# The recurrent unit's square root on GpSimd instead of ScalarE, with its factor in the next product

## The chip, the cores and the metric

The kernel runs on one core of a Trainium2 chip. A core has TensorE (PE in the profile), VectorE (DVE), ScalarE (ACT), GpSimd (POOL) and SyncE (SP), each with an instruction queue of its own, and 16 DMA engines. What is compared is the device time of one execution, in microseconds; less is better.

## What is computed

One inference step through two layers of a hybrid backbone, on 128 context tokens and 256 latent tokens with 1024 features. Each layer has a combined input projection, attention, a recurrent branch, a gated merge of the two and a mixture of 16 experts. The part that matters here is the recurrent branch:

```python
def _rglru_bidir(xr, lp, h0):
    xc = _conv_centred(xr, lp['conv_w'], lp['conv_b']).astype(F32)
    for d in range(2):
        r = jax.nn.sigmoid(_block_diag(xc, lp['lru_wa'][d], lp['lru_ba'][d]))
        i = jax.nn.sigmoid(_block_diag(xc, lp['lru_wx'][d], lp['lru_bx'][d]))
        log_a = -LRU_C * r * jax.nn.softplus(-lp['lru_lambda'][d])
        u = jnp.sqrt(-jnp.expm1(2.0 * log_a)) * (i * xc)
        h_last, y = _lru_scan(jnp.exp(log_a), u, h0[:, d], reverse=(d == 1))
    ...
```

The change is about the `sqrt` in `u`, which is taken over 2 directions x 1024 features x 384 tokens in each layer.

## The kernel before

Features lie on partitions, 128 at a time, and tokens along the free dimension: 384 columns, or 387 in the recurrent branch, where 3 columns part the two streams. A recurrent unit is one pair of direction d and feature tile j, so a layer has 16 of them (PAIRS, both directions of a tile in a row).

Every engine's program is written by hand, and semaphores order them. The stage of interest is a loop of 24 units i in each layer (from L632 on PE, L1057 on ACT, L1504 on DVE). In unit i PE computes the scores of attention unit i (a head and a block of 128 queries, L601 to L606), a product of the input projection (L471 for the first eight, L460 for the other sixteen), transposes the probabilities of unit i (L614), from unit 8 on computes the two gate products of recurrent pair n = i - 8 (L654), and then attends with the probabilities of unit i - 1 (L627). Every third attention unit is a context unit with 128 keys and no mask; the others have 384 keys.

ACT does in unit i: the exponential of the scores (L1003, L1005), from unit 9 on the root of pair i - 9 (lru_root, L1050), the Tanh of the product (L1079), the copy of the transposed probabilities (L1015), the gates' Tanh, the decay and its square for pair i - 8 (lru_tables, L1034 to L1044), and the copy of an attention output (L1020). Behind the loop come lru_root(15) and then the high parts of the next weights (high_part, L942).

DVE does in unit i: the maximum of the scores (L1427 to L1430), the norm of the probabilities (L1437 to L1439), in some units the split of a finished head into two parts (att_split, L1361 and L1362), and from unit 9 on one_minus_square (L1446), which makes the root's argument, and scan for pair i - 9. In scan L1453 multiplies the input by its gate, L1455 multiplies by the root, for which it waits, and L1463 scans the two streams. In a backward unit (d = 1) L1473 adds the two directions, L1477 multiplies by the other gate, and L1361 and L1362 split the result. Behind the loop stand one_minus_square(15), the low part of a weight split (low_part, L1372), the last attention split, another low part and scan(15). PE's first product of the attention projection (L471 again) needs the first weight split and the attention splits, the third needs its weight parts in a buffer that scan(15) still reads.

POOL loads the small gate weights of each pair by four DMAs (L1773) into one of two buffers, when the gate products of the pair before the last are done. ACT's functions need tables; the compiler puts a table load ahead of an activation whose function is not in the loaded set.

Of the kernel before, what the change touches and what calls it, by code (L numbers as in the profile page):

```python
# [11 lines left out]
ALU = mybir.AluOpType  # L12
ACT = mybir.ActivationFunctionType
AX = mybir.AxisListType

P = 128
D = 1024
KT = D // P
# [19 lines left out]
CW = CTX + SEG + LAT  # L38
# [123 lines left out]
def build(nc, x_prompt, x_sample, cache_k, cache_v, state_h, c, c_ctx, norm1_g, norm2_g, w_ada, b_ada,  # L162
# [4 lines left out]
    with ctx:  # L167
# [13 lines left out]
        def S(name):  # L181
            if name not in sems:
                sems[name] = ctx.enter_context(nc.semaphore(name))
            return sems[name]
# [684 lines left out]
        def _(ac):  # L869
# [56 lines left out]
            for l in range(DEPTH):  # L926
# [116 lines left out]
                        ac.wait_ge(S("lru_square"), m)  # L1043
                    ac.activation(a2, a, ACT.Square).then_inc(S("lru_act"), 1)  # L1044

                def lru_root(n):

                    ac.wait_ge(S("lru_square"), l * 16 + n + 1)
                    th = tmp[:, 2 + n % 2, :]
                    ac.activation(th, th, ACT.Sqrt, scale=0.25).then_inc(S("root_ready"), 1)  # L1050

                def gelu_tanh(j):
                    ac.wait_ge(S("gelu_arg"), l * KT + j + 1)
                    ac.activation(gelu_t[:, j % 2, :], gelu_t[:, j % 2, :], ACT.Tanh, scale=GELU_C)\
# [2 lines left out]
                for i in range(3 * KT):  # L1057
                    kind = ("gr", "ga", "gb")[i // KT]
                    j = i % KT
                    exps(i)  # L1060
                    if 1 <= i <= KT:
                        gelu_tanh(i - 1)
                    if i > KT:
                        lru_root(i - KT - 1)
                    if i + AHEAD < KT:
                        high_part(2 * KT + i + AHEAD)
                    if kind == "gr":
                        copy_out((l, kind, j), gr[:, j, :], T)
                        g_read(ac, (l, kind, j))
                        if l * KT + j >= 2:  # L1070
                            ac.wait_ge(S("gelu_done"), l * KT + j - 1)
                        if l and j == 0:
                            ac.wait_ge(S("lru_used"), l * 16)
                        ac.activation(gelu_t[:, j % 2, :], gr[:, j, :], ACT.Square).then_inc(S("gelu_sq"), 1)
                    else:
                        dst = ga if kind == "ga" else gb
                        g = (l, kind, j)
                        bank = g_ready(ac, g)
                        ac.activation(dst[:, j, :], bank[:, 0:T], ACT.Tanh, scale=0.5).then_inc(g_free(g), 1)  # L1079
                    pt_copy(i)  # L1080
                    if i in (3, 7):
                        ada_copy(l, 8 + i // 4)
                    if i >= KT:
                        lru_tables(i - KT)
                    if i >= 1:
                        att_copy(i - 1)
                lru_root(15)
                high_part(EARLY)
                att_copy(23)
                high_part(EARLY + 1)  # L1090
# [144 lines left out]
        def _(ve):  # L1235
            chain = [0]

            def link(ins):

                chain[0] += 1  # L1240
                ins.then_inc(S("dve_chain"), 1)
                ve.wait_ge(S("dve_chain"), chain[0])
                return ins
# [99 lines left out]
            for l in range(DEPTH):  # L1343
# [104 lines left out]
                def scan(n):  # L1448
                    d, j = PAIRS[n]
                    m = l * 16 + n  # L1450
                    a, th, ti = tmp[:, n % 2, :], tmp[:, 2 + n % 2, :], tmp[:, 4 + n % 2, :]

                    link(ve.scalar_tensor_tensor(ti, ti, 1.0, xc[:, j, :], ALU.add, ALU.mult))  # L1453
                    ve.wait_ge(S("root_ready"), m + 1)
                    link(ve.tensor_tensor(th, th, ti, ALU.mult))  # L1455
                    dst = hyb[:, :] if d == 0 else ti
                    for st in range(2):
                        cs = slice(0, CTX) if st == 0 else slice(LAT0, CW)
                        init = 0.0 if st == 0 else v_state(l, d, j)
                        aa, ww, oo = a[:, cs], th[:, cs], dst[:, cs]  # L1460
                        if d == 1:
                            aa, ww, oo = aa[:, ::-1], ww[:, ::-1], oo[:, ::-1]
                        ins = ve.tensor_tensor_scan(oo, aa, ww, init, ALU.mult, ALU.add)  # L1463
                    link(ins)
                    last = dst[:, CTX - 1:CTX] if d == 0 else dst[:, 0:1]
                    if l and n == 0:
                        ve.wait_ge(S("tran_done"), T_AT[(l - 1, "state", 0)] + 1)
                    ve.tensor_copy(hlast[:, d * 8 + j:d * 8 + j + 1], last).then_inc(S("hlast_ready"), 1)
                    if d == 1:

                        for st in range(2):
                            cs = slice(0, CTX) if st == 0 else slice(LAT0, CW)
                            ins = ve.tensor_tensor(th[:, cs], hyb[:, cs], ti[:, cs], ALU.add)  # L1473
                        link(ins)
                        for st in range(2):
                            cs = slice(0, CTX) if st == 0 else slice(LAT0, CW)
                            ins = ve.scalar_tensor_tensor(gr[:, j, STREAM[st]], gr[:, j, STREAM[st]], 0.5, th[:, cs],  # L1477
                                                          ALU.mult, ALU.mult)
                        link(ins)
                        halves(qT_r[:, j, :], gr_r[:, j, :], gr[:, j, :]).then_inc(S("rnn_ready"), 1)  # L1480
                    ve.wait_ge(S("hlast_ready"), m + 1)
                    ve.nop().then_inc(S("lru_used"), 1)
# [262 lines left out]
        @block.gpsimd  # L1745
        def _(po):
            po.memset(gatew[:, :, :, :], 0.0).then_inc(S("gatew_zero"), 1)
            po.wait_ge(S("gatew_zero"), 1)

            po.wait_ge(S("zeroed"), 1)  # L1750
            for b in range(MORE):
# [2 lines left out]
            for l in range(DEPTH):  # L1754
                def modulated(which):

                    base = (2 * l + which) * KT
                    for k in range(KT):
                        po.wait_ge(S("xn_ready"), base + k + 1)
                        po.tensor_scalar(hT[:, k, 0:CTX], hT[:, k, 0:CTX], modA[:, which, k, 0:1],  # L1760
                                         modT[:, which * 24 + k, 0:1], ALU.mult, ALU.add).then_inc(S("h_ready_p"), 1)

                po.wait_ge(S("first_mods"), l + 1)
                modulated(0)

                for n, (d, j) in enumerate(PAIRS):
                    m = l * 16 + n
                    if m >= 2:
                        q = m - 2
                        po.wait_ge(S("gemm_done"), G_AT[(q // 16, "gate_x", q % 16)] + 1)  # L1770
                    for which, w in enumerate((lru_wa, lru_wx)):
                        for half in range(2):
                            po.dma_start(gatew[half * 64:half * 64 + 64, which, n % 2, half * 64:half * 64 + 64],  # L1773
                                         w[l, d, 2 * j + half]).then_inc(S(f"gatew_loaded{n % 2}"), 16)
                modulated(1)
                t_read(po, (l, "ids", 0))
                po.wait_ge(S("h2_stored"), (l + 1) * TT * 16)
# [83 lines left out]
```

## Time and profile before

| | us |
|---|---|
| median of 3 runs | 1765.71 |
| lowest, highest | 1762.88, 1768.92 |
| span of the profiled execution | 1765.8 |
| PE busy | 1626.6 (92%) |
| DVE busy | 625.9 (35%) |
| ACT busy | 563.8 (32%) |
| POOL busy | 135.4 (8%) |

The stage of interest, units 8 to 23 of the loop, lies from about 221 to 348 us in the first layer and from about 1079 to 1206 us in the second. After each comes the attention projection. A busy share is an average over stages with different limits, so the rows below are mostly of one stretch. "Granted clock" (PEclk) is the share of TensorE's full clock that was granted.

### The profile page before, as it was taken

The numbers are of one execution on the slowest core, as the hardware profiler recorded it, in microseconds if no ns is written. First come the engines' busy times: TensorE is split into PE (matmuls) and PEld (weight loads), VectorE is DVE, ScalarE is ACT, GpSimd is POOL, SyncE is SP. The second block draws the span as 40 slices with busy tenths as digits, with TensorE's granted clock in tenths as the row PEclk, the third lists the DMA queues.
The fourth block names the chain that finished last, engine by engine and source line by source line (L and its number), as shares of the span: only waits on it lengthen the run. The fifth ranks groups of instructions, "written<-read, shape, count | busy, mean of one in ns | idle before, by whom it ended". The sixth has DMA issues, their size and how long they took to land.

```text
span 1765.8 us, 17572 instructions
## 1 busy us (share of the span) xinstructions
PE 1626.6 (92%) x6715; PEld 1075.4 (61%) x6715; DVE 625.9 (35%) x1459; ACT 563.8 (32%) x1021; POOL 135.4 (8%) x214
## 2 busy tenths in 40 slices
PE   4999999999959999999859999998995899999996
PEld 3599866589834444444358987667993444444445
DVE  3347666646440000000042665676555100000002
ACT  1233579932111111111122356995212111111112
POOL 0100022100010000000040001220001000000001
PEclk9799999989969999999979999998997899999998
DMA  9356431236458999998363552212505699999963
GB/s 353 112 207 224 148 103 56 95 104 226 169 201 291 336 333 339 335 337 325 144 218 136 203 190 100 101 60 97 191 1 226 215 338 335 337 334 337 336 219 132
DMA packets 132329, 377.08 MB, mean 214 GB/s; under 512 B 7816, under 2 KB 11280, under 8 KB 132240
## 3 DMA queue, kind: packets, MB, share of 16 engines
q1 hardware_dynamic: 112064, 326.04, 51.9%
q0 software_dynamic: 11152, 27.80, 4.2%
q10 hardware_dynamic: 9024, 22.03, 3.2%
q8 instruction: 59, 0.97, 0.2%
q14 instruction: 30, 0.25, 0.0%
HBM read 351.19 MB, written 24.66 MB: 213 GB/s over the span
## 4 chain that ended last, share of the span: by engine, by line
PE 85%; DVE 6%; ACT 4%; issue 3%; ACTq 1%; POOL 1%; DMA 1%; DVEq 0%; POOLq 0%
PE bank L739 25%; PE bank L471 22%; PE bank L750 12%; PE bank L460 9%; PE bank L481 2%; PE bank L654 2%; PE bank L731 2%; PE bank L830 1%; PE bank L497 1%; PE bank L490 1%; PE bank L627 1%; PE bank L564 1%; PE bank L559 1%; PE bank L785 1%; POOL hT L1760 1%
## 5 line engine op out<-in xcount | busy, mean ns | idle before, releaser
L739 PE MATMUL bank<-ring,ga 128*128 128x512 f32 x768 | 334.9, 592 | 0.0
L1691 DVE SCALAR_TENSOR_TENSOR gr<-gr,bank 128x512 f32<-128x512 f32 x32 | 22.0, 688 | 646.3 <-ACT gr L1144 646.3
L739 PEld LDWEIGHTS bank<-ring,ga 128*128 128x128 f32 x768 | 144.2, 190 | 173.2 <-issue 173.2
L460 PE MATMUL bank<-hT,ring 128*128 128x384 f32 x576 | 197.9, 499 | 19.5 <-POOL hT L1760 12.1
L471 PE MATMUL bank<-parts_r,ga_r 128*128 128x384 f32 x768 | 202.6, 345 | 0.0
L750 PE MATMUL bank<-ring,ga 128*128 128x512 f32 x384 | 168.9, 593 | 3.7 <-issue 3.7
L460 PEld LDWEIGHTS bank<-hT,ring 128*128 128x128 f32 x576 | 109.3, 195 | 91.6 <-issue 21.3
L1144 ACT ACTIVATE gr<-bank 128x512 f32<-128x512 f32 x32 | 19.1, 598 | 396.3 <-PE bank L739 396.3
L471 PEld LDWEIGHTS bank<-parts_r,ga_r 128*128 128x128 f32 x768 | 138.3, 188 | 5.9 <-issue 5.0
L471 PE MATMUL bank<-parts_r,gb_r 128*128 128x384 f32 x384 | 129.7, 338 | 0.0
L750 PEld LDWEIGHTS bank<-ring,ga 128*128 128x128 f32 x384 | 71.2, 190 | 85.4 <-issue 85.4
L739 PE MATMUL bank<-parts,ga 128*128 128x512 f32 x256 | 117.9, 615 | 2.3 <-ACT ga L1135 2.3
L471 PE MATMUL bank<-parts_r,hT_r 128*128 128x384 f32 x432 | 98.9, 356 | 9.1 <-DVE parts_r L1362 9.1
L1160 ACT ACTIVATE gb<-bank 128x512 f32<-128x512 f32 x64 | 34.7, 594 | 189.0 <-PE bank L750 189.0
L471 PEld LDWEIGHTS bank<-parts_r,hT_r 128*128 128x128 f32 x432 | 81.3, 199 | 12.8 <-DVE parts_r L1362 10.9
L739 PEld LDWEIGHTS bank<-parts,ga 128*128 128x128 f32 x256 | 49.9, 198 | 62.7 <-issue 59.6
L1372 DVE TENSOR_TENSOR gb_r<-ring,ga_r 128x1024 fp32r<-128x1024 f32 x48 | 58.5, 1222 | 53.1 <-ACT ga_r L942 51.5
L1780 POOL DMA_INDIRECT gr<-h_rows,ids x32 | 30.4, 949 | 587.6 <-PE bank L731 537.1
L471 PEld LDWEIGHTS bank<-parts_r,gb_r 128*128 128x128 f32 x384 | 72.1, 188 | 0.0
L1773 POOL DMA_DIRECT2D gatew<-in_lru_wa x64 | 33.9, 535 | 480.1 <-PE bank L654 480.0
L942 ACT ACTIVATE hT_r<-ring 128x1024 fp32r<-128x1024 f32 x32 | 33.8, 1057 | 78.0 <-PE bank L471 78.0
L750 PE MATMUL bank<-parts,ga 128*128 128x512 f32 x128 | 56.3, 592 | 0.0
(283 smaller groups left out, 2240.1 us busy)
## 6 DMA issues: line engine op xcount, KB each, us to landing
ring<-in_w_gate_up SPq DMA_DIRECT2D x48, 2048.0 KB, 9.8
ring<-in_w_ada SPq DMA_DIRECT2D x24, 2048.0 KB, 8.4
ring<-in_w_down SPq DMA_DIRECT2D x24, 2048.0 KB, 9.0
ring<-in_w_in SPq DMA_DIRECT2D x22, 2048.0 KB, 7.8
parts<-in_w_gate_up SPq DMA_DIRECT2D x16, 2048.0 KB, 9.8
parts<-in_w_down SPq DMA_DIRECT2D x8, 2048.0 KB, 8.9
expert_rows<-gb ACTq DMA_DIRECT2D x32, 512.0 KB, 8.2
ring<-in_w_attn_proj SPq DMA_DIRECT2D x4, 2048.0 KB, 8.3
```

Source lines behind the costliest of these rows:

```text
L460: mm = pe.matmul(bank[:, 0:width], slot_kn(slot)[:, k, n * P:(n + 1) * P], rhs(k), start=(k == 0), stop=(k == KT - 1))
L471: mm = pe.matmul(bank[:, 0:T], w[:, k, :], x[:, k, :], start=(k == 0 and i == 0), stop=(k == KT - 1 and i == 2))
L481: mm = pe.matmul(bank[g:g + 32, :], cpad[:, k, :], slot_kn(s)[:, k, :], start=(k < 4), stop=(k >= 4), tile_position=(0, g))
L654: pe.matmul(bank[:, 0:CW], gatew[:, which, n % 2, :], xc[:, j, :], start=True, stop=True).then_inc(S("gemm_done"), 1)
L731: mm = pe.transpose(dst_banks[i][:, k * CAP:(k + 1) * CAP], xrows[0:CAP, kk * P:(kk + 1) * P], ident[0:CAP, 0:CAP])
L739: mm = pe.matmul(G[n][0:CAP, :], xt[:, half * 4 + k, 0:CAP], slot_wide(slots[half])[:, k, n * 512:(n + 1) * 512], start=(half == 0 and k = ...
L750: mm = pe.matmul(SB[n][0:CAP, :], at[:, k, 0:CAP], slot_wide(slot)[:, k, n * 512:(n + 1) * 512], start=(k == 0), stop=(k == 3))
L942: ac.activation(w_part(kind, n)[0], slot_kn(s)[:, :, n % 4 * P:(n % 4 + 1) * P], ACT.Copy)\
L1160: ins = ac.activation(yo[e % 2][0:CAP, i * 512:(i + 1) * 512], SB[i][0:CAP, :], ACT.Copy)
L1372: ve.tensor_tensor(low, slot_kn(s)[:, :, n % 4 * P:(n % 4 + 1) * P], high.bitcast(F32), ALU.subtract)\
L1773: po.dma_start(gatew[half * 64:half * 64 + 64, which, n % 2, half * 64:half * 64 + 64], w[l, d, 2 * j + half]).then_inc(S(f"gatew_loaded{n ...
L1780: po.indirect_dma_start(out=dst, out_offset=None, in_=h2d[:, :], in_offset=bass.IndirectOffsetOnAxis(ap=idx, axis=0)).then_inc(sem, 16)
```

## The change

ACT no longer takes the root. POOL takes it, as the argument to the power of 0.5, with the exponent read from a column that is set once at the start. ACT's root included a factor of one quarter under the root; DVE's next product now multiplies by 0.5. On POOL the root of pair n - 2 stands behind the gate loads of pair n, and the last two behind all loads.

```diff
-                def lru_root(n):
-
-                    ac.wait_ge(S("lru_square"), l * 16 + n + 1)
-                    th = tmp[:, 2 + n % 2, :]
-                    ac.activation(th, th, ACT.Sqrt, scale=0.25).then_inc(S("root_ready"), 1)
-
...
                     exps(i)
                     if 1 <= i <= KT:
                         gelu_tanh(i - 1)
-                    if i > KT:
-                        lru_root(i - KT - 1)
...
-                lru_root(15)
                 high_part(EARLY)
...
                     ve.wait_ge(S("root_ready"), m + 1)
-                    link(ve.tensor_tensor(th, th, ti, ALU.mult))
+                    link(ve.scalar_tensor_tensor(th, th, 0.5, ti, ALU.mult, ALU.mult))
...
             po.memset(gatew[:, :, :, :], 0.0).then_inc(S("gatew_zero"), 1)
-            po.wait_ge(S("gatew_zero"), 1)
+            po.memset(nrt[:, 1:2], 0.5).then_inc(S("gatew_zero"), 1)
+            po.wait_ge(S("gatew_zero"), 2)
...
+                def lru_root(n):
+
+                    po.wait_ge(S("lru_square"), l * 16 + n + 1)
+                    th = tmp[:, 2 + n % 2, :]
+                    po.tensor_tensor(th, th, nrt[:, 1:2].broadcast_to([P, CW]), ALU.pow).then_inc(S("root_ready"), 1)
...
                             po.dma_start(gatew[half * 64:half * 64 + 64, which, n % 2, half * 64:half * 64 + 64],
                                          w[l, d, 2 * j + half]).then_inc(S(f"gatew_loaded{n % 2}"), 16)
+                    if n >= 2:
+                        lru_root(n - 2)
+                lru_root(14)
+                lru_root(15)
                 modulated(1)
```

On ACT a unit of the loop (here from the exponential of one unit to the gates of the next) reads before:

```order
L1003 ACTIVATE pr,smx<-bank,smx 128x384
L1005 ACTIVATE smx<-sinkb,smx 128x1
L1050 ACT_TABLE_LOAD
L1050 ACTIVATE tmp<-tmp 128x387
L1079 ACT_TABLE_LOAD
L1079 ACTIVATE ga<-bank 128x384
L1015 ACTIVATE pt<-bank 128x384
L1034 ACTIVATE tmp<-bank,hb 128x387
```

The same place now, with the lines of the changed kernel:

```order
L1003 ACTIVATE pr,smx<-bank,smx 128x384
L1005 ACTIVATE smx<-sinkb,smx 128x1
L1071 ACTIVATE ga<-bank 128x384
L1015 ACTIVATE pt<-bank 128x384
L1034 ACTIVATE tmp<-bank,hb 128x387
```

The root and both table loads are gone from the unit. In the whole order of ACT 70 table loads stand before and 10 now; L916, the root of the normalisation in the middle of a layer, has one ahead of it now that it had not.

On POOL, in the same loop, the gate loads of successive pairs stand alone before:

```order
L1773 DMA gatew<-in_lru_wa 64x64 [waits gemm_done]
L1773 DMA gatew<-in_lru_wa 64x64
L1773 DMA gatew<-in_lru_wx 64x64 x2
L1773 DMA gatew<-in_lru_wa 64x64 [waits gemm_done]
```

Now a root, which waits for DVE, stands between them:

```order
L1771 DMA gatew<-in_lru_wa 64x64 [waits gemm_done]
L1771 DMA gatew<-in_lru_wa 64x64
L1771 DMA gatew<-in_lru_wx 64x64 x2
L1762 TENSOR_TENSOR tmp<-tmp,nrt 128x387 [waits lru_square]
L1771 DMA gatew<-in_lru_wa 64x64 [waits gemm_done]
```

The 16 roots of a layer are 16 such rows. The orders of PE and SP are the same, and on DVE only the form of L1455 changes.

## Rows read from the trace of the kernel before

**Rows 1.** The page, busy time of each engine.

```profile
PE 1626.6 (92%) x6715; PEld 1075.4 (61%) x6715; DVE 625.9 (35%) x1459; ACT 563.8 (32%) x1021; POOL 135.4 (8%) x214
```

**Rows 2.** Busy time by stretch: start:end, length, PE, PEld, DVE, ACT, POOL, clock, DMA.

```profile
229.90:341.50 111.60, 109.89 (x427) 70.34 (x425) 77.78 (x214) 102.55 (x194) 28.57 (x56) 1.00 0.19 65
341.50:357.60 16.10, 9.21 (x37) 5.99 (x36) 9.29 (x24) 14.64 (x26) 0.00 (x0) 0.85 0.37 130
357.60:394.00 36.40, 36.40 (x196) 36.13 (x200) 19.06 (x28) 8.50 (x8) 0.00 (x0) 0.92 0.33 116
```

**Rows 3.** Timeline, products of units 9, 22 and 23: start us, length, engine.

```profile
229.91 5.33 PE L460 MATMUL bank<-hT,ring 128*128 128x384 f32 x16
...
333.74 5.33 PE L460 MATMUL bank<-hT,ring 128*128 128x384 f32 x16
...
341.47 5.43 PE L460 MATMUL bank<-hT,ring 128*128 128x384 f32 x16
```

**Rows 4.** Groups by line on ACT: count, then busy us, mean ns, idle before.

```profile
L1050 ACT ACT_TABLE_LOAD x32 | 41.1, 1283 | 0.6
L1079 ACT ACT_TABLE_LOAD x30 | 38.5, 1283 | 0.5
...
L1050 ACT ACTIVATE tmp<-tmp 128x387 f32<-128x387 f32 x32 | 16.9, 527 | 13.0 <-DVE tmp L1446 12.5
```

**Rows 5.** Timeline of DVE, the end of unit 10 and unit 11.

```profile
245.33 0.15 DVE L1468 COPY hlast<-tmp 128x1 f32<-128x1 f32 x1
...
247.59 0.29 DVE L1427 TENSOR_TENSOR bank<-bank,con 128x128 f32<-128x128 f32 x1
247.91 0.56 DVE L1428 TENSOR_REDUCE smx<-bank 128x1 f32<-128x384 f32 x1
...
250.37 0.35 DVE L1361 CAST parts_r<-qT 128x384 fp32r<-128x384 f32 x1
...
251.24 0.56 DVE L1446 SCALAR_TENSOR_TENSOR tmp<-tmp 128x387 f32<-128x387 f32 x1
251.71 0.56 DVE L1453 SCALAR_TENSOR_TENSOR tmp<-tmp,xc 128x387 f32<-128x387 f32 x1
252.46 0.56 DVE L1455 TENSOR_TENSOR tmp<-tmp 128x387 f32<-128x387 f32 x1 [0.19 <-ACT tmp L1050]
...
254.16 0.15 DVE L1468 COPY hlast<-hyb 128x1 f32<-128x1 f32 x1
254.46 0.29 DVE L1428 TENSOR_REDUCE smx<-bank 128x1 f32<-128x128 f32 x1
```

**Rows 6.** Groups by line on ACT, the exponential of long and context units.

```profile
L1003 ACT ACTIVATE pr<-bank,smx 128x384 f32<-128x384 f32 x32 | 18.5, 579 | 29.5 <-DVE smx L1430 29.5
...
L1003 ACT ACTIVATE pr<-bank,smx 128x128 f32<-128x128 f32 x16 | 5.8, 363 | 9.3 <-DVE smx L1430 9.3
```

**Rows 7.** Timeline, from unit 23 on DVE to the attention projection.

```profile
343.67 0.29 DVE L1427 TENSOR_TENSOR bank<-bank,con 128x128 f32<-128x128 f32 x1
...
348.88 0.49 ACT L1079 ACTIVATE gb<-bank 128x384 f32<-128x384 f32 x1
...
349.37 0.15 DVE L1468 COPY hlast<-hyb 128x1 f32<-128x1 f32 x1
...
355.43 1.22 DVE L1372 TENSOR_TENSOR hT_r<-ring,hT_r 128x1024 fp32r<-128x1024 f32 x1 [2.38 <-ACT hT_r L942]
...
357.57 7.33 PE L471 MATMUL bank<-parts_r,hT_r 128*128 128x384 f32 x26 [3.32 <-DVE parts_r L1362]
...
359.17 0.56 DVE L1455 TENSOR_TENSOR tmp<-tmp 128x387 f32<-128x387 f32 x1
...
363.89 1.22 DVE L1372 TENSOR_TENSOR xc_r<-ring,xc_r 128x1024 fp32r<-128x1024 f32 x1 [0.69 <-ACT xc_r L942]
```

**Rows 8.** Groups by line, two of POOL's and DVE's reciprocal.

```profile
L1760 POOL TENSOR_SCALAR hT<-hT,modA,modT x32: 444/448/1942, 55.9 to 1341.8; 128x128 f32<-128x128 f32 x32
...
L1847 POOL MEMSET const-float32-1.0<- 128x1 f32 x1 | 0.1, 102 | 0.0
...
L1341 DVE RECIPROCAL hyb<-hyb 128x384 f32<-128x384 f32 x4 | 10.2, 2552 | 14.3 <-ACT hyb L916 14.3
```

## The prediction

> **What bounds the kernel now.** I read the page's busy shares first: TensorE (PE) is busy 92% of the span, the others far less [rows 1]. So a change on ACT, VectorE (DVE) or POOL counts only where PE waits for them. The root is taken 16 times in each of the two layers, in units 8 to 23 of the stage that interleaves attention, the gate products and the recurrent unit, so I read that stretch next. From 229.9 to 341.5 us PE is busy 109.89 of 111.60 us and ACT 102.55, DVE 77.78 and POOL 28.57 [rows 2]: PE is the bound and ACT runs close behind it. From 341.5 to 357.6 PE is busy only 9.21 of 16.10 us, while ACT is busy 14.64: this tail waits for others. The products L460, one a unit, start at a pace of (341.47 - 229.91) / 14 = 7.97 us; 341.47 - 333.74 = 7.73 us is a unit in which PE waited for nothing [rows 3].
>
> **What the change takes from ACT.** The root needs another table than Tanh and Exp. Rows show 32 loads before the root (1283 ns each) and 30 before the next Tanh, and 32 roots of 527 ns [rows 4]. The two loads and the root make 1.28 + 1.28 + 0.53 = 3.1 us of a unit's 8 us. In the order of the changed kernel 60 of the 70 table loads are gone (the 62, less two that now stand ahead of the normalisation's root at L916, which in the kernel before found the table already loaded). So 60 x 1.283 + 32 x 0.527 = 94 us leave ACT. The two new loads cost nothing: they can run while ACT waits for the square sums there.
>
> What this alone can give PE is small. The loop can fall from 7.97 to 7.73 us a unit: 14 x 0.24 = 3.3 us. In the tail the last Tanh of gb runs at 348.88, where the product before it ends near 341.47 + 5.3 = 346.8: 2.1 us go there. The load and the root, 1.28 + 0.53 us ahead of the first weight split, go too [rows 4, 7]; some of that is hidden, and I take 3.5 us. Together 6.8 us a layer, 13.6 us at most, if the root costs nothing elsewhere.
>
> **What it puts on the path of DVE.** DVE computes the root's argument (L1446), one product beside the root (L1453), and then waits for the root (L1455). Behind that wait on DVE's queue stand the scan and then the softmax maximum of the next unit, and PE's transposes wait for the softmax. How long DVE's unit is when neither ACT nor PE holds it up can be read from 247.59 to 254.46 us: 6.87 us, of which 0.87 are an attention split (250.37 to 251.24) that 7 of the 14 units 9 to 22 have [rows 5]. So 6.00 us. A unit with the backward direction adds the sum of both directions and its split, (247.59 - 245.33) - (254.46 - 254.16) = 1.96 us, 7 times. A context unit has no mask (0.29), half the maximum (0.56 - 0.29) and a shorter exponential (0.579 - 0.363) and norm, about 0.9 us less, 5 times [rows 5, 6]. The mean is 6.00 + (7 x 1.96 - 5 x 0.9 + 7 x 0.87) / 14 = 7.09 us. DVE is only 0.9 us a unit from being the bound. In its unit the root counts in full: from L1446's start (251.24) to L1455's (252.46) are 1.22 us, of which 0.56 the argument, 0.53 the root and 0.13 the handovers; L1453 beside it hides all but the 0.19 us that DVE idled. If the root takes R us on POOL, with the same handovers, the unit takes 7.09 - 0.53 + R = 6.56 + R.
>
> The path of one layer runs from the start of unit 9 on DVE (about 230.2, 0.3 us behind its product at 229.91) to the first product of the attention projection at 357.57, 127.4 us now. After the change: fourteen units at 6.56 + R; unit 23 up to its L1468 at (349.37 - 343.67) - 0.53 + R = 5.17 + R; 0.2 us to the next L1446 and 0.47 (251.24 to the start of its successor) until the weight split; and from that split L1372 to PE 357.57 - 355.43 = 2.14 [rows 3, 5, 7]. Sum: 99.8 + 15 R. **The change per layer is 15 R - 27.6 us**, not below -6.8, since PE's own work bounds there. Layer 1 runs the same instructions, so I double it. Break-even is R = 1.84 us.
>
> The last root (n = 15) runs beside the weight split and the attention split. But the third product of the projection needs a split that waits for the scan behind it: ready at R + 0.69 + 5.94 us after L1446's start (363.89 + 1.22 - 359.17 is the 5.94), wanted at 2.6 + 8.9 (two products of 24 matmuls, 48 x 36.40 / 196). That is R - 4.9 us more a layer when R is above 4.9 [rows 2, 7].
>
> POOL's queue: root n stands between the gate loads for n + 2 and for n + 3, and PE wants the latter two units after that root. POOL is busy 28.57 of 111.60 us with nothing else in the loop [rows 2], so they stay hidden: only from a root longer than a unit on would they come late, and the unit itself contains the root. The factor moved into the next DVE product costs nothing: L1446 has that form already and takes 0.56 us, as L1455 does [rows 5]. The memset at the start is 0.1 us, beside loads.
>
> **The unknown: R.** No row shows a power on POOL. Low end: the nearest row is its multiply-and-add with 128 columns, 448 ns at the median; less about 100 for a one-column memset that is 2.7 ns a column, or 387 x 2.7 + 100 = 1.15 us [rows 8]. Middle row: DVE's reciprocal of 128x384, a function that is iterated, takes 2.55 us against 0.56 for a product [rows 5, 8]. High end: a power of an arbitrary exponent is a logarithm, a product and an exponential. I count 36 arithmetic steps (14 for each series, 8 for taking exponents apart and joining them); at 1.35 ns a step and column, half of POOL's row, that is 387 x 36 x 1.35 ns + 100 = 18.9 us. I take the middle by ratio between 2.55 and 18.9, R = 7 us, since an iterated function is dearer than simple arithmetic on every engine shown here but ACT, which has tables, and POOL has shown none. An estimate for simple arithmetic from the Trainium skill (GPSIMD Engine Reference, Elementwise — side-by-side cycle accounting: 2.6 cycles an element at 1.2 GHz) would be 0.84 us, with which the change would win its 13.6 us; the row's 2.7 ns a column, 3.2 cycles, is near it, but both are for arithmetic, not for a power.
>
> **Forecast.** R = 7: 15 x 7 - 27.6 + 2.1 = 79.5 us a layer, 159 in all; 1765.8 (the profiled span, which equals the median of 1765.71) + 159 = 1925 us. The unit then takes 13.6 us, of which the root 7.
>
> **Rivals.**
> (a) The root is nearly as cheap as arithmetic, R under 1.66. DVE stays within or close to PE's unit, ACT's relief shows, and the gain decides: at R = 1.15, 1765.8 - 13.6 = 1752 us. For it: POOL's row, and ACT's busy share. Against it: what a power is.
> (b) R between 1.66 and 2.02: the tail's gain and the loop's loss cancel, within 5.3 us of 1765.8.
> (c) POOL overlaps the steps of a power. At R = 4 the unit is 10.6 us: 60 - 27.6 = 32.4 a layer, 1831 us; the reciprocal's 2.55 us would give 1787. For it: much of POOL's 448 ns may be fixed or memory cost, so that a step is cheaper than half of it. Against it: nothing here shows the overlap. The Trainium skill (GPSIMD Engine Reference, the same section) states roughly 3 operations a cycle for longer bodies: 36 steps would be 12 cycles a column, an estimate of 3.9 us, near 1828 us. No row here shows it.
> (d) R above 15: at 18.9, 283.5 - 27.6 + 14 = 270 a layer, 2306 us.
> (e) With the forecast's R, PE's clock falls: PE works 7.7 of 13.6 us, and in the tail now, where it is busy 9.21 of 16.10 us, its granted clock is 0.85 [rows 2]. At the lower level of 1.2 GHz a unit's 7.7 us become 15.4, more than 13.6: up to 1.8 x 15 x 2 = 54 us more, 1979. I count it within the forecast's case, which it only moves.
> (f) The tables are loaded as before: the change would not do what it says. The order excludes it.
>
> **How the numbers follow.** R from 5 to 15 (1861 to 2181 us): 0.47. (d): 0.12. (c), R from 2.02 to 5: 0.25. (b): 0.04. (a): 0.12. Faster by over 0.3% (5.3 us, about what a measurement of this kernel can tell from no change) is (a), 0.12; within it (b), 0.04; slower the rest, 0.84. The range takes in everything from (a)'s 1752 us to R = 15, 225 - 27.6 + 10.1 = 207.5 a layer, 2181 us; it leaves out (d), 0.12.
>
> **What would show it.** The duration of POOL's new row, which is R; DVE's idle time before the product behind the root (L1455 here), 0.19 - 0.53 + R = R - 0.34 each time; the distance of product starts, 6.6 + R where that is above 7.7; ACT 94 us less busy; no table load between the units; PE's granted clock in the stage. If R is large and the stage does not lengthen by 15 R - 27.6, my DVE path is wrong. If R is small and PE still gains nothing, the price of the tail is.

## The result, and the profile after

The changed kernel takes 3704.84 us (median, 3704.07 to 3706.42) where the kernel before, on the same chip, takes 1766.20: 2.0985 times as long, with a 95% interval of 2.0953 to 2.1016. The forecast of 1925 us and its upper end of 2181 us were both far too low. The profiled execution spans 3704.3 us against 1765.8, so 1938.5 us are to be found, 969.3 in each of the two layers.

The page of the kernel after: busy time of each engine, then from the table of 40 slices the rows of PE, POOL and TensorE's clock in tenths, then the shares of the chain of work that ended last. They answer to [rows 1].

```profile
PE 1698.8 (46%) x6715; PEld 1120.1 (30%) x6715; DVE 626.0 (17%) x1459; ACT 478.1 (13%) x929; POOL 2131.3 (58%) x247
...
PE   6961211211211158999889311121110201879998
...
POOL 1049999999998930000010799899999999010000
PEclk8985655655655579999989665565565555889999
...
POOL 54%; PE 35%; DVE 6%; issue 2%; ACT 1%; ACTq 1%; DMA 0%; DVEq 0%; POOLq 0%
```

PE had 92% of the span and now has 46%. POOL went from 135.4 us to 2131.3, and the last chain runs over it for 54% of the span. The slices show where: two blocks, one for each layer, in which POOL stands at 9 and PE at 1 or 2. The page's costliest groups (busy us, mean ns, then the idle time of the engine just before them and what ended it) name the instruction:

```profile
L1762 POOL TENSOR_TENSOR tmp<-tmp,nrt 128x387 f32<-128x387 f32 x32 | 1995.5, 62358 | 142.0 <-DVE tmp L1437 142.0
...
L1446 DVE SCALAR_TENSOR_TENSOR tmp<-tmp 128x387 f32<-128x387 f32 x32 | 18.0, 563 | 1979.2 <-POOL tmp L1762 1979.2
```

One root of 128x387 takes R = 62.36 us on POOL, and DVE's product behind it (L1455 before, L1446 now) waited 1979.2 us for the 32 of them, where each wait before was like the 0.19 us of [rows 5]. The timeline from the end of unit 13 to the root of unit 14 shows one turn of the loop (start, length, engine, and in brackets the idle time before and who ended it):

```profile
574.97 0.56 DVE L1446 SCALAR_TENSOR_TENSOR tmp<-tmp 128x387 f32<-128x387 f32 x1 [62.04 <-POOL tmp L1762]
...
576.96 0.30 DVE L1418 TENSOR_TENSOR bank<-bank,con 128x128 f32<-128x128 f32 x1
...
579.75 0.55 DVE L1437 SCALAR_TENSOR_TENSOR tmp<-tmp 128x387 f32<-128x387 f32 x1
...
579.98 0.88 PE L614 MATMUL bank<-con,pr 128*128 128x128 f32 x3 [58.28 <-DVE pr L1430]
...
580.22 0.55 DVE L1444 SCALAR_TENSOR_TENSOR tmp<-tmp,xc 128x387 f32<-128x387 f32 x1
580.39 62.31 POOL L1762 TENSOR_TENSOR tmp<-tmp,nrt 128x387 f32<-128x387 f32 x1 [3.46 <-DVE tmp L1437]
```

The root's result lets DVE do the scan and then the softmax of the next unit. That softmax lets PE go on, and right behind it DVE makes the argument of the next root. So PE waits some 58 us in each unit. The products L460 of units 10 to 16 answer to [rows 3]:

```profile
238.67 5.33 PE L460 MATMUL bank<-hT,ring 128*128 128x384 f32 x16
307.65 5.66 PE L460 MATMUL bank<-hT,ring 128*128 128x384 f32 x16
377.66 5.33 PE L460 MATMUL bank<-hT,ring 128*128 128x384 f32 x16
445.90 5.33 PE L460 MATMUL bank<-hT,ring 128*128 128x384 f32 x16
516.22 5.48 PE L460 MATMUL bank<-hT,ring 128*128 128x384 f32 x16
584.88 5.33 PE L460 MATMUL bank<-hT,ring 128*128 128x384 f32 x16
653.66 5.33 PE L460 MATMUL bank<-hT,ring 128*128 128x384 f32 x16
```

They start (653.66 - 238.67) / 6 = 69.17 us apart, where they started 7.97 us apart before. A window inside the loop of the first layer (start:end, length, busy PE, PEld, DVE, ACT, POOL, granted clock, DMA share, GB/s) answers to [rows 2]:

```profile
290.00:1170.00 880.00, 132.62 (x393) 83.33 (x393) 73.08 (x200) 60.40 (x143) 821.75 (x66) 0.58 0.03 11
```

PE is busy for 15% of it, with a granted clock of 0.58, near the lower of its two levels (1.2 and 2.4 GHz). In the whole run PE is busy 1698.8 - 1626.6 = 72 us longer for the same 6715 instructions. Within the loop this costs nothing, since PE waits in every unit anyway; behind it a few us are lost, as shown further on.

### The profile page after: what moved, and what is told of

It is laid out like the page before. It is cut to its first block, busy times and chain, and to the rows that moved or that the text cites. A ratio compares the mean times of both kernels' runs of the same rounds, so it can differ in the third digit from the quotient of the medians.

```text
span 3704.3 us, 17513 instructions
## 1 busy us (share of the span) xinstructions
PE 1698.8 (46%) x6715; PEld 1120.1 (30%) x6715; DVE 626.0 (17%) x1459; ACT 478.1 (13%) x929; POOL 2131.3 (58%) x247
## 4 chain that ended last, share of the span: by engine, by line
POOL 54%; PE 35%; DVE 6%; issue 2%; ACT 1%; ACTq 1%; DMA 0%; DVEq 0%; POOLq 0%
POOL tmp L1762 54%; PE bank L739 12%; PE bank L471 10%; PE bank L750 6%; PE bank L481 1%; PE bank L460 1%; PE bank L731 1%; PE bank L830 1%; PE bank L497 1%; PE bank L490 1%; DVE tmp L1446 0%; DVE tmp L1454 0%; DVE smx L1419 0%; DVE hyb L1454 0%; DVE tmp L1437 0%
## 5 line engine op out<-in xcount | busy, mean ns | idle before, releaser
L1762 POOL TENSOR_TENSOR tmp<-tmp,nrt 128x387 f32<-128x387 f32 x32 | 1995.5, 62358 | 142.0 <-DVE tmp L1437 142.0
L614 PE MATMUL bank<-con,pr 128*128 128x128 f32 x112 | 29.5, 372 | 1650.7 <-DVE pr L1430 1650.7
L614 PEld LDWEIGHTS bank<-con,pr 128*128 128x128 f32 x112 | 17.0, 187 | 1669.4 <-issue 1668.8
L1446 DVE SCALAR_TENSOR_TENSOR tmp<-tmp 128x387 f32<-128x387 f32 x32 | 18.0, 563 | 1979.2 <-POOL tmp L1762 1979.2
L1003 ACT ACTIVATE pr<-bank,smx 128x384 f32<-128x384 f32 (+1 forms) x48 | 24.4, 509 | 1754.9 <-DVE smx L1421 1754.9
L460 PE MATMUL bank<-hT,ring 128*128 128x384 f32 x576 | 198.9, 501 | 16.1 <-POOL hT L1752 12.0
L1752 POOL TENSOR_SCALAR hT<-hT,modA,modT 128x128 f32<-128x128 f32 x32 | 23.2, 738 | 317.9 <-DVE hT L1339 266.6
L739 PEld LDWEIGHTS bank<-ring,ga 128*128 128x128 f32 x768 | 144.2, 190 | 173.1 <-issue 173.1
L471 PE MATMUL bank<-parts_r,hT_r 128*128 128x384 f32 x432 | 99.8, 358 | 123.9 <-DVE parts_r L1353 123.9
L460 PEld LDWEIGHTS bank<-hT,ring 128*128 128x128 f32 x576 | 111.8, 200 | 87.4 <-issue 22.8
L739 PE MATMUL bank<-parts,ga 128*128 128x512 f32 x256 | 117.3, 612 | 2.4 <-ACT ga L1126 2.4
L471 PE MATMUL bank<-parts_r,xc_r 128*128 128x384 f32 x240 | 49.3, 366 | 111.1 <-DVE xc_r L1363 111.1
```

The lines of the kernel that those rows point to most:

```text
L460: mm = pe.matmul(bank[:, 0:width], slot_kn(slot)[:, k, n * P:(n + 1) * P], rhs(k), start=(k == 0), stop=(k == KT - 1))
L471: mm = pe.matmul(bank[:, 0:T], w[:, k, :], x[:, k, :], start=(k == 0 and i == 0), stop=(k == KT - 1 and i == 2))
L614: mm = pe.transpose(bank[:, i * P:(i + 1) * P], pr[:, u % 2, i * P:(i + 1) * P], ident)
L739: mm = pe.matmul(G[n][0:CAP, :], xt[:, half * 4 + k, 0:CAP], slot_wide(slots[half])[:, k, n * 512:(n + 1) * 512], start=(half == 0 and k = ...
L1762: po.tensor_tensor(th, th, nrt[:, 1:2].broadcast_to([P, CW]), ALU.pow).then_inc(S("root_ready"), 1)
```

## Experiments

The theory was the prediction's own rule: per layer 15 R - 27.6 us, not below -6.8, and R - 4.9 more when R is above 4.9, with R alone mis-sized. The first rival was that something other than R makes up part of the lost time (the handover to POOL, the late gate loads behind the root, a clock that falls). The second was that the added factor or the moved queue costs time of its own.

### The root left out

```diff
-                    po.tensor_tensor(th, th, nrt[:, 1:2].broadcast_to([P, CW]), ALU.pow).then_inc(S("root_ready"), 1)
+                    po.nop().then_inc(S("root_ready"), 1)
```

> The changed kernel with the root left out on every engine: POOL only hands the argument on, so the recurrent values are without their root. ACT is relieved of its 32 roots and 60 table loads as in the changed kernel, and R, the time between DVE's argument and its product, is near 0. Theory (15 R - 27.6 us a layer, not below -6.8): PE's own work bounds, 1766 - 13.6 = 1752 us, products 7.7 us apart. Rival, that ACT's relief is worth nothing since PE bounds the stage already: 1766 us, no difference.

Measured: 1752.68 us against 1765.94, ratio 0.9928 (0.9911 to 0.9944). Everything of the change is in this kernel but the arithmetic, and it gains 13.3 us, as the -6.8 us a layer said. Its trace has the parts as well: in the first layer unit 23's product starts 108.57 us behind unit 9's where it was 111.56, and the first product of the attention projection 12.62 us behind that where it was 16.11. So the loop gives 3.0 us and the tail 3.5, for the 3.3 and 3.5 of the prediction. Neither the handovers, nor the gate loads, nor the factor cost anything that shows.

### A multiplication in place of the power

```diff
-                    po.tensor_tensor(th, th, nrt[:, 1:2].broadcast_to([P, CW]), ALU.pow).then_inc(S("root_ready"), 1)
+                    po.tensor_tensor(th, th, nrt[:, 1:2].broadcast_to([P, CW]), ALU.mult).then_inc(S("root_ready"), 1)
```

> The changed kernel with a multiplication by the same broadcast column in place of the power (the values are wrong for that); all else, the form of the instruction and its operands, is the same. Theory (the power function is the cost, not POOL, the handover or the broadcast operand): the POOL row takes about 1 us, between 0.84 and 1.15, and the time is 1752 us. Rival (POOL's tensor by tensor form with a broadcast operand is what is slow): the row stays near 62 us and the time near 3705 us.

Measured: 1753.1 us, ratio 0.9922 (0.9902 to 0.9942). POOL's group, and the window of the loop:

```profile
L1762 POOL TENSOR_TENSOR tmp<-tmp,nrt 128x387 f32<-128x387 f32 x32 | 33.9, 1059 | 109.9 <-DVE tmp L1437 109.9
```

```profile
229.90:341.50 111.60, 111.53 (x435) 71.58 (x434) 80.82 (x222) 66.33 (x158) 43.87 (x69) 1.00 0.20 65
```

The same form of instruction, with the same operands, takes 1.06 us as a multiplication and 62.36 as a power. With 1.06 us PE is busy for 111.53 of 111.60 us: this is the prediction's rival (a), at its price of 1752. So the place on POOL and the form are cheap, and the power is what costs. The fastest of the 32 rows has 832 ns, the median 1074 ns; the last section shows where the difference comes from. The Trainium skill (GPSIMD Engine Reference, Elementwise — side-by-side cycle accounting) gives 2.6 cycles an element for two inputs, at 1.2 GHz an estimate of 0.84 us. For a multiplication that nothing holds up the trace agrees.

### Chains of three and seven multiplications

```diff
-                    po.tensor_tensor(th, th, nrt[:, 1:2].broadcast_to([P, CW]), ALU.pow).then_inc(S("root_ready"), 1)
+                    for _ in range(6):
+                        po.tensor_tensor(th, th, nrt[:, 1:2].broadcast_to([P, CW]), ALU.mult).then_inc(S("pool_chain"), 1)
+                        pool_links[0] += 1
+                        po.wait_ge(S("pool_chain"), pool_links[0])
+                    po.tensor_tensor(th, th, nrt[:, 1:2].broadcast_to([P, CW]), ALU.mult).then_inc(S("root_ready"), 1)
```

The other kernel has range(2). These set R to middling values, where the rule turns.

> As e1_mult, but three multiplications one after the other, each waiting for the last, so that R is about 3.3 us. Theory: the path through DVE bounds, 15 x 3.3 - 27.6 = 22 us a layer more, 1810 us. Rival (POOL's work hides until it is as long as PE's unit of 7.7 us): 1752 us, as e1_mult.

> As e1_mult, but seven multiplications in a row, so that R is about 7.4 us, the place of the forecast. Theory: 15 x 7.4 - 27.6 + 2.5 = 86 us a layer, 1938 us. Rival (hidden until 7.7 us): near 1755 us. A second rival, that the lower granted clock lets PE bound the loop: up to 54 us on top, 1992 us, with a granted clock near 0.5 in the stage and no idle PE.

Measured: 1806.12 us for three, ratio 1.0224 (1.0206 to 1.0241), and 1913.72 for seven, ratio 1.0842 (1.0824 to 1.0861). The timeline of one chain of seven (six, then the last), and a window over most of the loop of that kernel:

```profile
270.25 5.62 POOL L1764 TENSOR_TENSOR tmp<-tmp,nrt 128x387 f32<-128x387 f32 x6 [2.56 <-DVE tmp L1437]
...
275.95 0.83 POOL L1767 TENSOR_TENSOR tmp<-tmp,nrt 128x387 f32<-128x387 f32 x1
```

```profile
246.00:427.00 181.00, 121.98 (x406) 76.67 (x404) 79.27 (x212) 65.14 (x151) 109.68 (x146) 0.86 0.15 51
```

R is 275.95 + 0.83 - 270.25 = 6.53 us, less than the 7.4 that I expected: only the first multiplication takes 1.07 us, the six behind it 0.83 each. With 6.53 the rule gives 15 x 6.53 - 27.6 + 1.6 = 72.0 us a layer, 144 in all. The span grew from 1765.8 to 1911.7, by 145.9; by the medians it is 147.8. PE is busy 122 of 181 us at a clock of 0.86: it is not the bound, so the fallen clock doesn't set the pace at this R. For three multiplications R is 2.89 us, the rule gives 31.5, and the span grew by 39.8. Most of the missing 8 us lies on the rule's own path: from the product of unit 9 to the first product of the attention projection the trace has 146.6 us where it had 127.7, so 19.0 more in each layer, and the rule gives 15.8. PE is busy 12.0 us longer than before in that kernel, so near the turning point the clock may cost something; the runs don't separate that from an error in the 27.6.

### Half the columns, 8 of 128 partitions, exponent 1

```diff
-                    po.tensor_tensor(th, th, nrt[:, 1:2].broadcast_to([P, CW]), ALU.pow).then_inc(S("root_ready"), 1)
+                    po.tensor_tensor(th[:, 0:194], th[:, 0:194], nrt[:, 1:2].broadcast_to([P, 194]), ALU.pow).then_inc(S("root_ready"), 1)
```

```diff
-                    po.tensor_tensor(th, th, nrt[:, 1:2].broadcast_to([P, CW]), ALU.pow).then_inc(S("root_ready"), 1)
+                    po.tensor_tensor(th[0:8, :], th[0:8, :], nrt[0:8, 1:2].broadcast_to([8, CW]), ALU.pow).then_inc(S("root_ready"), 1)
```

```diff
-            po.memset(nrt[:, 1:2], 0.5).then_inc(S("gatew_zero"), 1)
+            po.memset(nrt[:, 1:2], 1.0).then_inc(S("gatew_zero"), 1)
```

> The changed kernel with the power over 194 of the 387 columns (the other columns keep the argument). If the power costs by the column, the row falls from 62.3 to 31.2 us and the time by 31.1 us x 16 a layer (15 in the loop, one behind it), to about 3704 - 995 = 2709 us. Rival (a fixed cost of each instruction, such as code that is loaded each time): the row stays near 62 us and the time near 3705.

> The changed kernel with the power over 8 of the 128 partitions (the others keep the argument), 387 columns. If the partitions of a column are computed together, the row stays at 62 us and the time at 3705. If they are computed one after the other within groups of 16, the row halves to about 31 us and the time is about 2710; if all 128 were one after the other, it would be about 4 us.

> The changed kernel with an exponent of 1 in place of one half (the root is left out of the values). If the power is computed by the same general steps whatever the exponent, the row stays at 62.3 us and the time at 3705 us. Rival (the cost is that of a fractional exponent, and whole ones take a short way): a row of a few us, and a time below 1900 us.

Measured, one run each: 2719.9, 3706.1 and 3704.2 us. The power's row in these three kernels, in the same order (shortest/median/longest in ns, first and last start):

```profile
L1762 POOL TENSOR_TENSOR tmp<-tmp,nrt x32: 31542/31566/32212, 231.5 to 2134.2; 128x194 f32<-128x194 f32 x32
```

```profile
L1762 POOL TENSOR_TENSOR tmp<-tmp,nrt x32: 62288/62319/62956, 235.1 to 3090.3; 8x387 f32<-8x387 f32 x32
```

```profile
L1762 POOL TENSOR_TENSOR tmp<-tmp,nrt x32: 62295/62321/62963, 233.4 to 3088.9; 128x387 f32<-128x387 f32 x32
```

193 columns less take (62.32 - 31.57) / 193 = 159.3 ns a column away, and 62.32 - 387 x 0.1593 = 0.7 us is left as fixed cost (a line through two sizes). Sixteen times fewer partitions take nothing away: the cost goes by column, and using fewer partitions with the same columns doesn't help. An exponent of one costs the same as one half, so neither exponent tried here has a short way. The rule holds for half the columns too: 2 x (16 x 31.57 - 32.5) = 945 us against 2717.7 - 1765.8 = 952 measured.

### The factor alone

In the kernel before, with the root still on ACT:

```diff
-                    ac.activation(th, th, ACT.Sqrt, scale=0.25).then_inc(S("root_ready"), 1)
+                    ac.activation(th, th, ACT.Sqrt).then_inc(S("root_ready"), 1)
...
-                    link(ve.tensor_tensor(th, th, ti, ALU.mult))
+                    link(ve.scalar_tensor_tensor(th, th, 0.5, ti, ALU.mult, ALU.mult))
```

> The kernel before with only the other part of the change: ACT takes the root without the quarter, and DVE's product multiplies by 0.5. Theory: both forms of the product take 0.56 us, so the time is that of before, 1766 us within 3 us. Rival (the form with three operands is slower on DVE): 32 roots by the difference of the rows, visible if over 0.1 us each.

Measured: 1768.04 us, ratio 1.0007 (0.9996 to 1.0018): no difference. The product's row has the same 564 ns as before:

```profile
L1455 DVE SCALAR_TENSOR_TENSOR tmp<-tmp 128x387 f32<-128x387 f32 x32 | 18.0, 564 | 7.0 <-ACT tmp L1050 6.9
```

### Looking for the gain without POOL: the tail

Without its arithmetic the change is worth 13 us. Part of that should be had on ACT itself. First only the tail: in the kernel before, the last root moved behind the weight split that PE waits for.

```diff
-                lru_root(15)
                 high_part(EARLY)
                 att_copy(23)
                 high_part(EARLY + 1)
+                lru_root(15)
```

> The kernel before with one change of order on ACT: the last root of a layer stands behind the two weight splits (high parts) and the attention copy between them, not ahead of them. Theory (the table load and the root, 1.28 + 0.53 us, stand on the path to the first product of the attention projection): that product starts about 1.8 us earlier in each layer, 1766 - 3.6 = 1762 us, ratio 0.998. Rival (the last root's scan then comes late and holds up the third product): no gain, 1766 us or a little more.

Measured: 1765.29 us, ratio 1.0003 (0.9992 to 1.0014). That is a miss. The trace has the step where it was looked for: the last product of the loop and the first of the attention projection start

```profile
337.02 5.43 PE L460 MATMUL bank<-hT,ring 128*128 128x384 f32 x16
351.31 1.01 PE L471 MATMUL bank<-parts_r,hT_r 128*128 128x384 f32 x2 [1.36 <-DVE parts_r L1362]
```

14.29 us apart, where they were 357.57 - 341.47 = 16.10 before [rows 3, 7], and the second layer has the same step. Twice 1.8 us should have shown as 3.6, and the interval reaches only to 1.4. The same traces show where most of it went in this execution. Within the second attention projection stands a PE instruction that starts at 1240.0 us in the kernel before. From there PE takes 525.3 us to its last instruction, where the kernel before takes 522.1. About 1.5 us of that are lost in one short stretch. Both windows start at the same place of the program, first in this kernel, then in the kernel before (start:end, length, busy PE, PEld, DVE, ACT, POOL, granted clock, DMA share, GB/s):

```profile
1285.70:1289.10 3.40, 3.40 (x12) 3.40 (x12) 0.00 (x0) 0.00 (x0) 0.00 (x0) 0.51 0.00 0
1293.90:1297.50 3.60, 3.60 (x22) 3.60 (x21) 0.31 (x2) 0.25 (x1) 0.00 (x0) 1.00 0.00 0
```

PE is busy throughout in both, at a granted clock of 0.51 here and 1.00 there, the lower and the higher level. What made the clock fall there, and whether it does so in each execution, no run shows. The span of this profile, 1760.7 us, isn't the gain either: PE stands 4.6 us earlier at unit 9 (225.34 against 229.91), before anything that was moved has run.

### Roots in pairs

Two roots in a row need one pair of table loads. This costs a third set of buffers (partly in memory of the input xp, which DVE clears again behind the loop) and a scan one unit later:

```diff
-                    if i > KT:
-                        lru_root(i - KT - 1)
+                    if i >= KT + 2 and i % 2 == 0:
+                        lru_root(i - KT - 2)
+                        lru_root(i - KT - 1)
...
+                lru_root(14)
                 lru_root(15)
                 high_part(EARLY)
...
-                        scan(i - KT - 1)
+                    if i > KT + 1:
+                        scan(i - KT - 2)
```

> The kernel before with the roots left on ACT but taken two at a time, in every second unit, behind one table load; the scan of a pair comes one unit later, for which a third set of buffers is used. 38 table loads in place of 70. Theory: the wait for a root no longer falls in each unit, ACT is relieved of about 1.3 us a unit, and the last Tanh of the loop has no load ahead of it: up to 3.3 us in the loop and 2.1 in the tail of each layer, 1766 - 11 = 1755 us. Rival (two scans behind the loop hold up the third product of the attention projection and the loop's gain is given back): 1766 us.

Measured: 1765.04 us, ratio 0.9993 (0.9982 to 1.0004), no gain, the rival's number. ACT has 38 table loads in place of 70 and is busy 525.2 us in place of 563.8. But the loop's products start 7.90 us apart, (340.97 - 230.33) / 14, barely under 7.97: in the even units load, two roots and load still stand together ahead of the Tanh that frees PE's bank.

```profile
256.86 1.28 ACT L1056 ACT_TABLE_LOAD   x1
258.16 0.94 ACT L1056 ACTIVATE tmp<-tmp 128x387 f32<-128x387 f32 x2
259.12 1.28 ACT L1086 ACT_TABLE_LOAD   x1
260.41 0.49 ACT L1086 ACTIVATE ga<-bank 128x384 f32<-128x384 f32 x1
```

And two scans stand behind the loop on DVE, so the third product of the attention projection waits 0.79 us, the rival's reason:

```profile
355.94 6.08 PE L477 MATMUL bank<-parts_r,hT_r 128*128 128x384 f32 x26 [4.32 <-DVE parts_r L1370]
...
366.67 4.45 PE L477 MATMUL bank<-parts_r,xc_r 128*128 128x384 f32 x24 [0.79 <-DVE xc_r L1380]
```

But this wait doesn't explain the missing gain. Counted from unit 9's product, the third product starts 366.67 - 230.33 = 136.3 us later where it was 138.7 before, so 2.3 us are won in spite of it, and as much in the second layer. What is won is lost further on: in this trace PE takes 524.3 us from that instruction at 1240 us to its last, against 522.1 before, again with a stretch at the lower clock in the midst of products (1290.6 to 1294.0 us, granted clock 0.50), and 0.9 us more between the two layers' loops.

### Roots in pairs, the last pair behind the weight splits

Against the kernel with pairs:

```diff
-                lru_root(14)
-                lru_root(15)
                 high_part(EARLY)
                 att_copy(23)
                 high_part(EARLY + 1)
+                lru_root(14)
+                lru_root(15)
```

> As e9_pairs, and the last two roots stand behind the two weight splits on ACT. Theory: 1.3 + 1.1 us less ahead of the attention projection in each layer than e9_pairs, if the scans behind it are not late: 1751 us. Rival (the scans are late then): as e9_pairs or slower.

Measured: 1757.45 us against 1765.38, ratio 0.9957 (0.9943 to 0.9972). This kernel leaves nothing out and is faster than both kernels, than the one before by 7.9 us; the 1751 us of its forecast were still 6 too low. Its timeline from the last product of the loop:

```profile
336.35 5.43 PE L466 MATMUL bank<-hT,ring 128*128 128x384 f32 x16 [0.17 <-ACT gb L1086]
...
348.27 1.28 ACT L1056 ACT_TABLE_LOAD   x1
...
349.07 7.16 PE L477 MATMUL bank<-parts_r,hT_r 128*128 128x384 f32 x26 [2.07 <-DVE parts_r L1370]
349.57 0.94 ACT L1056 ACTIVATE tmp<-tmp 128x387 f32<-128x387 f32 x2
...
359.93 4.33 PE L477 MATMUL bank<-parts_r,xc_r 128*128 128x384 f32 x24
```

The table load and the two roots run while PE works on the first two products, and the third starts without an idle time before it. The projection starts 349.07 - 336.35 = 12.72 us behind the last product, 3.4 less than before, and the loop gives 14 x 0.07 = 1.0: twice 4.4 is 8.8, near the 7.9 measured. From the instruction at 1240 us on PE takes 522.5 us here, so next to nothing is given back. The move that brought nothing alone is here the one that brings out the pairs' gain: 2.3 us in each tail against the pairs alone, and 1.8 us from 1240 us on, where the stretch at the lower clock is absent, which nothing in the edit promised.

## Why the prediction was wrong

**The step that failed** is "The unknown: R". It ended at 18.9 us, from 36 arithmetic steps at 1.35 ns a column, and took 7 us as the middle. R is 62.36 us, 161 ns a column, 3.3 times that end and 9 times that middle. Even at the whole 2.7 ns of POOL's row [rows 8] 36 steps make 97 ns a column. Against the fastest multiplications here, 0.83 us, a power is worth 62.36 / 0.83 = 75 of them. So the count of steps that one would write by hand was no upper bound for what the engine does. How many steps the power really takes, and how long one of them is, no run shows; that part of the cause stays open. Nor was the reciprocal's 2.55 us on DVE a near row: it is another engine's, and halving the way to it by ratio made R look known. That the exponent may be arbitrary explains nothing here, since an exponent of one costs the same.

**Rival (d)** had the sign and the mechanism, with a chance of 0.12. Its price of 2306 us stood at the same end of 18.9 and fell with it. Rival (c) pointed away from it: its R = 4 was 16 times too low. Beside it stood the Trainium skill's roughly 3 operations a cycle (GPSIMD Engine Reference, Elementwise — side-by-side cycle accounting), with an estimate of 3.9 us for 36 steps. The trace doesn't bear that out for a power counted as 36 steps.

**The rule held**, but for a few us. With the measured R it gives 15 x 62.36 - 27.6 + 62.36 - 4.9 = 965.3 us a layer, 1930.5 in all; measured are 1938.5. Across the kernels, the change of the profiled span against 1765.8 us, and of the medians against the kernel before on the same chip:

| kernel | R, us | rule, us | span, us | medians, us |
|---|---|---|---|---|
| root left out | 0 | -13.6 | -16.0 | -13.3 |
| one multiplication | 1.06 | -13.6 | -13.7 | -12.8 |
| three | 2.89 | +31.5 | +39.8 | +40.2 |
| seven | 6.53 | +144 | +145.9 | +147.8 |
| power, 194 columns | 31.57 | +945 | +951.9 | +954.4 (one run) |
| power, 387 columns | 62.36 | +1930.5 | +1938.5 | +1938.6 |

The spans are of single executions, and these differ by up to 4.6 us ahead of the loop: in the chain of seven PE stands at 226.55 us at unit 9, 3.4 earlier than before. By the medians the rule is 4 to 9 us short wherever the root bounds. On its path, from unit 9's product to the first product of the projection, it is short by 3.2, 3.0, 2.2 and 1.9 us in the first layer of the last four kernels.

**Its steps one by one.** The unit: 6.56 + 62.36 = 68.9 us, measured 69.17. DVE's idle time before the product behind the root: R - 0.34 = 62.02, measured 62.04. The last root, beside the weight split: the tail of the first layer shows it.

```profile
1264.87 0.56 DVE L1437 SCALAR_TENSOR_TENSOR tmp<-tmp 128x387 f32<-128x387 f32 x1
...
1265.51 62.96 POOL L1762 TENSOR_TENSOR tmp<-tmp,nrt 128x387 f32<-128x387 f32 x1 [2.74 <-DVE tmp L1437]
1266.48 0.99 DVE L1352 CAST parts_r<-qT 128x384 fp32r<-128x384 f32 x1
...
1268.11 7.60 PE L471 MATMUL bank<-parts_r,hT_r 128*128 128x384 f32 x26 [60.29 <-DVE parts_r L1353]
...
1334.57 0.69 PE L471 MATMUL bank<-parts_r,xc_r 128*128 128x384 f32 x1 [54.99 <-DVE xc_r L1363]
```

The first product of the projection starts 1268.11 - 230.77 = 1037.3 us behind the product of unit 9, and 99.8 + 15 R with the 0.3 to DVE's start is 1035.5. The third waits 54.99 us, where R - 4.9 gave 57.5. Answering to [rows 4], the 62 table loads of the roots and of the Tanh behind them are gone, and the normalisation's line has 4 in place of 2 (L916 here):

```profile
L916 ACT ACT_TABLE_LOAD x4 | 5.1, 1283 | 0.1
```

ACT's busy time fell by 563.8 - 478.1 = 85.7 us, not 94. The lengths of all its rows in the trace fell by 619.9 - 523.5 = 96.4 us, as worked out; but rows overlap, busy time counts an overlap once, and ACT's rows overlap less now, 45 us in place of 56. It was off the path. The factor is free, as the run with it alone shows. The gate loads stayed hidden: the gate products (L654) show no wait for POOL in the trace. The price of the tail and of the table switches, 13.6 us, was right: 13.3 and 12.8 us by the medians of the two kernels with a cheap "root".

**The clock, point (e),** fell as feared, and further, to 0.58 in the loop. It was to cost up to 54 us; in the loop it costs nothing, since at 69 us a unit even a slow PE is done in time. Behind the loop it makes up some of the 8 us that the rule leaves over: from the third product of the projection on, PE takes 17.4 us for what took 15.2, and 17.0 for 14.3 in the second layer, with this clock at the start of it:

```profile
1334.50:1352.60 18.10, 18.04 (x91) 18.04 (x92) 8.55 (x11) 3.83 (x4) 0.00 (x0) 0.87 0.33 117
```

## What to carry to other kernels

When the one unknown of a sum is the duration of an operation that no row shows, the range is that unknown's range: give its upper end as a factor over the nearest row of the same engine, and don't close it with a count of steps. Here the factor over the 1.15 us from POOL's row was 54; a run with the one operation in place would have told it. For this root ACT, which has it in a table, is the place: POOL takes some 118 times ACT's 527 ns for it [rows 4]. What the move was after, fewer table switches in front of the path, was to be had on ACT by taking two roots at a time and putting the last ones behind what PE waits for.

## What was not expected of the hardware

A power on POOL costs 0.7 us and 159.3 ns a column, whatever the partitions (8 or 128) or the exponent (0.5 or 1), where a multiplication of the same operands takes 0.83 us when DVE does nothing beside it.

DVE beside it matters. In the two kernels with chains 244 of POOL's multiplications run while DVE is idle, and each takes 0.83 us. The first of a chain starts while DVE's product L1444, which has two inputs, is still running, and takes 1.07 us; so do 30 of the 32 single ones. The other two, the last root of each layer, start while DVE is idle and keep 0.83 us; there it is DVE's next product with two inputs (L1363, at 349.07 us in the first layer) that takes 1.44 us in place of 1.22. So it isn't that POOL is slow on the first instruction after a pause: where two instructions overlap once, the one that starts second loses. Where DVE's work runs beside the chain for longer, in the tail of the chain of seven, both engines lose:

```profile
424.42 7.55 POOL L1764 TENSOR_TENSOR tmp<-tmp,nrt 128x387 f32<-128x387 f32 x6 [2.75 <-DVE tmp L1437]
425.39 0.99 DVE L1352 CAST parts_r<-qT 128x384 fp32r<-128x384 f32 x1
426.41 1.07 DVE L1353 TENSOR_TENSOR parts_r<-qT,parts_r 128x384 fp32r<-128x384 f32 x1
...
429.18 1.19 DVE L1444 SCALAR_TENSOR_TENSOR tmp<-tmp,xc 128x387 f32<-128x387 f32 x1
```

The six multiplications take 7.55 us where they took 5.62 at 270.25. The medians of the three DVE rows, in the same kernel, are 0.35, 0.56 and 0.56 us.

A power disturbs DVE far less. Of DVE's 16 casts of this line, the longest in the kernel with the power is

```profile
L1352 DVE CAST parts_r<-qT x16: 351/353/989, 233.7 to 3091.5; 128x384 fp32r<-128x384 f32 x16
```

989 ns against a median of 353, once in each layer, and it is the one that runs while POOL takes the last root (1266.48, above). That power is the long one as well, 62.96 us against a median of 62.32: both lost 0.64 us. DVE's products with two inputs that run beside the same power, L1353 and L1444 behind the cast, keep their 0.56 us. The Trainium skill (GPSIMD Engine Reference, Key points) says that the two engines share their interfaces to on-chip memory and names as contending DVE instructions in a 2-port mode or with two inputs. For POOL's multiplications the trace agrees, 1.07 against 0.83 us beside a product with two inputs; beside a power such products show no slowing, and that the cast runs in a 2-port mode no row here shows.
